# Delta-rule recurrence of an RWKV-7 layer: the doubling levels regrouped over the four quadrants of TensorE

## The reference

```python
def step(state, inp):
    r_t, w_t, k_t, v_t, kk_t, a_t = inp
    sa = jnp.einsum('bhvk,bhk->bhv', state, -kk_t)
    state = (state * w_t[:, :, None, :]
             + sa[..., None] * (kk_t * a_t)[:, :, None, :]
             + v_t[..., None] * k_t[:, :, None, :])
    y = jnp.einsum('bhvk,bhk->bhv', state, r_t)
    return state, y
...
_, y = lax.scan(step, state0, xs)
mu_y = jnp.mean(y, axis=-1, keepdims=True)
var_y = jnp.mean(jnp.square(y - mu_y), axis=-1, keepdims=True)
y = (y - mu_y) * lax.rsqrt(var_y + GN_EPS)
y = y * gn_g.reshape(H, N).astype(f32) + gn_b.reshape(H, N).astype(f32)
y = y + jnp.sum(rh * kh * r_k.astype(f32), axis=-1, keepdims=True) * vh
y = y.reshape(B, S, D).astype(h.dtype) * g
return y @ w_o
```

## Time and profile before

| what | value |
|---|---|
| median of 3 runs | 2886.83 us (2880.5 to 2887.5) |
| span of the profiled execution | 2890.0 us |
| level phases of the 8 pairs, first and last start of L3849 | 1697.1 and 2076.9 us |
| TensorE busy over the span | 2784.7 us (96%) |
| VectorE, GpSimd, ScalarE busy | 1962.0, 1435.9, 1370.0 us |

### The profile page before, as it was taken

The page is one execution under the profiler, slowest core; times in us unless marked ns, Lnnn a source line. Parts: engine busy times, 40 slices in busy tenths (PEclk is TensorE's granted clock), DMA queues, the critical chain, the costliest instruction groups (busy, mean ns, idle before and its releaser), DMA issues.

```text
span 2890.0 us, 63578 instructions
## 1 busy us (share of the span) xinstructions
PE 2784.7 (96%) x25936; PEld 2218.1 (77%) x25936; DVE 1962.0 (68%) x2814; ACT 1370.0 (47%) x2296; POOL 1435.9 (50%) x961
## 2 busy tenths in 40 slices
PE   8898899999999999998999999999999999999998
PEld 6544567887888888876678878988878788888887
DVE  6587888689777777788132347776647766656667
ACT  5476877235334433346433345666414443334445
POOL 0001000233777767774446636675552576677772
PEclk9899999999999999999999999999999999999999
DMA  8200000532332322331442411222312112111111
GB/s 300 77 1 16 1 2 2 212 106 62 88 102 73 93 81 83 93 113 32 160 146 88 161 60 55 76 85 64 112 36 59 44 48 69 44 44 58 57 45 73
DMA packets 194397, 225.29 MB, mean 78 GB/s; under 512 B 14862, under 2 KB 151649, under 8 KB 194209
## 3 DMA queue, kind: packets, MB, share of 16 engines
q1 hardware_dynamic: 182529, 180.66, 20.2%
q10 hardware_dynamic: 11680, 42.01, 4.0%
HBM read 185.15 MB, written 37.22 MB: 77 GB/s over the span
## 4 chain that ended last, share of the span: by engine, by line
PE 72%; DVE 9%; ACT 4%; issue 3%; POOL 2%; DMA 0%; ACTq 0%; DVEq 0%; SPq 0%; POOLq 0%
PE ps L148 18%; PE ps L149 18%; PE ps L150 18%; PE ps L3849 3%; DVE uc L1090 2%; PE ps L3858 2%; PE ps L2304 2%; PE ps L2293 1%; PE ps L2315 1%; PE ps L3778 1%; PE ps L3856 1%; ACT d_r L2446 1%; PE ps L3838 1%; DVE d_r L2706 1%; POOL w_lo L738 1%
## 5 line engine op out<-in xcount | busy, mean ns | idle before, releaser
L148 PE MATMUL ps<-x_hi,w_hi 128*128 128x512 f32 x1160 | 453.3, 391 | 2.9 <-POOL w_lo L738 2.8
L150 PE MATMUL ps<-x_hi,w_lo 128*128 128x512 f32 x1160 | 451.5, 389 | 0.0
L149 PE MATMUL ps<-x_lo,w_hi 128*128 128x512 f32 x1160 | 451.4, 389 | 0.0
L738 POOL TENSOR_TENSOR w_lo<-w_room,w_hi 128x512 fp32r<-128x512 f32 x188 | 287.7, 1543 | 232.4 <-ACT w_hi L1252 232.4
L738 POOL TENSOR_TENSOR w_lo<-sq_room,w_hi 128x512 fp32r<-128x512 f32 x182 | 285.8, 1581 | 218.9 <-ACT w_hi L1252 218.9
L1090 DVE SCALAR_TENSOR_TENSOR uc<-u,pc,uc 128x1024 f32<-128x1024 f32 x176 | 327.4, 1871 | 25.9 <-ACT uc L1266 15.6
L1078 DVE TENSOR_TENSOR u<-u,ps 128x512 f32<-128x512 f32 x228 | 151.1, 683 | 195.3 <-PE ps L150 170.9
L148 PEld LDWEIGHTS ps<-x_hi,w_hi 128*128 128x128 f32 x1160 | 217.7, 188 | 50.5 <-POOL w_lo L738 5.7
L148 PE MATMUL ps<-g_hi,w_hi 128*128 128x512 f32 x640 | 250.3, 391 | 6.5 <-DVE h L1156 6.2
L150 PEld LDWEIGHTS ps<-x_hi,w_lo 128*128 128x128 f32 x1160 | 217.7, 188 | 45.6
L149 PEld LDWEIGHTS ps<-x_lo,w_hi 128*128 128x128 f32 x1160 | 217.8, 188 | 44.8
(11 more groups left out here) (493 smaller groups left out, 6876.2 us busy)
## 6 DMA issues: line engine op xcount, KB each, us to landing
w_room<-in_f_w_up_dram SPq DMA_DIRECT2D x48, 512.0 KB, 5.0
rwkv_scratch<-rp_stage ACTq DMA_DIRECT2D x48, 512.0 KB, 3.5
sq_room<-in_f_w_up_dram SPq DMA_DIRECT2D x40, 512.0 KB, 4.6
ada_w<-in_ada_w_dram SPq DMA_DIRECT2D x80, 256.0 KB, 2.8
rc_raw<-rwkv_scratch SPq DMA_DIRECT2D x28, 512.0 KB, 3.9
d_ada_w<-in_ada_w_dram SPq DMA_DIRECT2D x24, 512.0 KB, 7.7
d_r<-in_ada_w_dram ACTq DMA_DIRECT2D x24, 512.0 KB, 6.4
sq_room<-in_f_w_down_dram SPq DMA_DIRECT2D x24, 512.0 KB, 4.4
```

The source lines that it names most:

```text
L148: pe.matmul(out, w_hi, x_hi, start=first, stop=False, skip_group_check=skip)
L149: pe.matmul(out, w_hi, x_lo, start=False, stop=False, skip_group_check=skip)
L150: return pe.matmul(out, w_lo, x_hi, start=False, stop=last, skip_group_check=skip)
L738: pool.tensor_tensor(slot_of(k.w_lo, s), src, slot_of(k.w_hi, s).bitcast(F32), ALU.subtract).then_inc(w_lo_done, 1)
```

## The change

It rearranges the levels. The second head's blocks 4 to 7 keep their l on the other partition half (`far`), so that the two halves of that head use different quadrants. A trip of TensorE's loop now has six groups of 16 matmuls, each over four quadrants: u and l of head 0 for blocks 0 to 3, the same for blocks 4 to 7, u of head 1, the next z of head 0 with l of head 1 for blocks 0 to 3, the same for blocks 4 to 7, and the next z of head 1. The loop is rotated: the first z stands ahead of it (`first_z`), the last u behind it (`last_u`), and it has four trips. ScalarE copies u and l of a whole head at a time, VectorE masks z of head 0 in two pieces and z of head 1 in one. Banks are dealt out anew, and so the sums of `kk*kk` go to halves of banks 2 and 3, and 5 and 6, and their reading (`max_dve`) stands ahead of the levels. On VectorE s1 moves behind level 1 and s2 behind level 4; on ScalarE `log_act` and `root_act` move from behind level 3 into level 5, between the copies of u of head 0 and head 1, and `turn_act` behind level 5. The diff, cut to its core:

```diff
     def max_dve(dve, q, i):
         dve.wait_ge(sem["sum"], 2 * q + i + 1)
-        dve.tensor_scalar(kk[:, halves(i)], bank(6 + i), 1e-24, None, ALU.max).then_inc(sem["max"], 1)
+        dve.tensor_scalar(kk[:, halves(i)].rearrange("p (b c) -> p b c", b=2), sums_of(q, i), 1e-24, None, ALU.max
+                          ).then_inc(sem["max"], 1)
...
         for i in range(2):
-            pe.matmul(bank(6 + i), same[:, :], kk[:, halves(i)], start=True, stop=True).then_inc(sem["sum"], 1)
+            if q >= 2 and i:
+                pe.wait_ge(sem["y_sb"], q - 1)
+            for n in range(2):
+                cols = slice((2 * i + n) * 2 * P, (2 * i + n + 1) * 2 * P)
+                last = pe.matmul(sums_of(q, i)[:, n, :], same[:, :], kk[:, cols], start=True, stop=True)
+            last.then_inc(sem["sum"], 1)
...
+    def far(h, x, c):
+        return c if h and x >= QUARTER else 1 - c
+
+    def z_of(pe, h, x, c):
+        i = x // QUARTER
+        out = bank(4 + i if h else 4 + 2 * i)[:, part(x, 1 - h if i == 0 else 0)]
+        return pe.matmul(out[hs(far(h, x, c)), :], tg[hs(c), x, h, G_M, :], ul[hs(c), 0, h, x, :],
+                         start=True, stop=True)
...
+    def first_z(pe, p):
+        for i in range(2):
+            if i and p + 1 < PAIRS:
+                pe.wait_ge(sem["max"], 2 * p + 4)
+            for x in quarter(i):
+                for c in range(2):
+                    a_last = z_of(pe, 0, x, 1 - c)
+                    if i:
+                        z_of(pe, 1, x, c)
+            a_last.then_inc(sem["z_ps"][0], 1)
+        pe.wait_ge(sem["z_sb"][0], 10 * p + 1)
+        for x in quarter(0):
             for c in range(2):
-                last = pe.matmul(bank(4 + h)[hs(1 - c), at(x)], tg[hs(c), x, h, G_M, :], ul[hs(c), 0, h, x, :],
-                                 start=True, stop=True)
-        last.then_inc(sem["z_ps"][h], 1)
+                last = z_of(pe, 1, x, c)
+        last.then_inc(sem["z_ps"][1], 1)
...
     def level_pe(pe, p, lv):
-        for h in range(2):
-            pe.wait_ge(sem["u_sb"][h], lv + 5 * p)
+        pe.wait_ge(sem["l_sb"][0], lv + 4 * p)
+        for i in range(2):
+            pe.wait_ge(sem["z_sb"][0], lv * 2 + (10 * p + i - 1))
+            pe.wait_ge(sem["l_sb"][1], lv * 2 + (8 * p + i - 1))
             begun(pe)
-            level_z(pe, h)
-        for h in range(2):
-            pe.wait_ge(sem["l_sb"][h], lv + 4 * p)
-            pe.wait_ge(sem["z_sb"][h], lv + 5 * p)
+            ul_a(pe, i)
+        pe.wait_ge(sem["z_sb"][1], lv + 5 * p)
+        begun(pe)
+        u_b(pe)
+        for i in range(2):
+            pe.wait_ge(sem["u_sb"][0], lv * 2 + (10 * p + i - 1))
             begun(pe)
-            level_ul(pe, h)
+            z_a_l_b(pe, i)
+        pe.wait_ge(sem["u_sb"][1], lv + 5 * p)
+        pe.wait_ge(sem["z_sb"][0], lv * 2 + (10 * p + 1))
+        begun(pe)
+        z_b(pe)
...
+            last_opened(pe, p)
             if p + 1 < PAIRS:
                 sums_pe(pe, p + 1)
...
             banks_opened(pe, p)
-            with pe.Fori(1, 6) as lv:
+            first_z(pe, p)
+            with pe.Fori(1, LV[-1]) as lv:
                 level_pe(pe, p, lv)
+            last_u(pe, p)
             if p + 1 < PAIRS:
                 bon_pe(pe, p + 1)
             tail_pe(pe, p)
...
             for lv in LV:
-                for s in range(2):
-                    levels_act(act, p, lv, s)
-                    if more and (lv, s) in ((1, 1), (2, 1)):
-                        ln_act(act, q, lv - 1)
-                    if p and (lv, s) == (3, 1):
-                        log_act(act, p - 1)
-                        root_act(act, p - 1)
-                    if more and (lv, s) in ((3, 1), (4, 1)):
-                        rs_act(act, q, lv - 3)
-                    if (lv, s) == (2, 1):
-                        turn_act(act, p, 0)
-                        turn_act(act, p, 1)
+                u_act(act, p, lv, 0)
+                if p and lv == LV[-1]:
+                    log_act(act, p - 1)
+                    root_act(act, p - 1)
+                u_act(act, p, lv, 1)
+                if lv < LV[-1]:
+                    la_act(act, p, lv)
+                    lb_act(act, p, lv)
+                if more and lv in (1, 2):
+                    ln_act(act, q, lv - 1)
+                if more and lv in (3, 4):
+                    rs_act(act, q, lv - 3)
+                if lv == LV[-1]:
+                    turn_act(act, p, 0)
+                    turn_act(act, p, 1)
             tail_act(act, p)
...
-            if p:
+            if more:
                 for i in range(2):
-                    s1_dve(dve, p - 1, i)
+                    max_dve(dve, q, i)
             for lv in LV:
-                for s in range(2):
-                    levels_dve(dve, p, lv, s)
-                    if more and (lv, s) == (1, 1):
-                        max_dve(dve, q, 0)
-                        max_dve(dve, q, 1)
-                    if p and (lv, s) == (3, 1):
-                        s2_dve(dve, p - 1, 0)
-                        s2_dve(dve, p - 1, 1)
-                    if p + 2 < PAIRS and (lv, s) == (2, 1):
-                        scan_dve(dve, p + 2, 0)
-                        scan_dve(dve, p + 2, 1)
+                for h in range(2):
+                    levels_dve(dve, p, lv, h)
+                if p and lv == 1:
+                    for i in range(2):
+                        s1_dve(dve, p - 1, i)
+                if p + 2 < PAIRS and lv in (2, 3):
+                    scan_dve(dve, p + 2, lv - 2)
+                if p and lv == 4:
+                    for i in range(2):
+                        s2_dve(dve, p - 1, i)
```

More of the change, by code:

```diff
@@ L101, in alloc @@
     k.nm_small = [k.sb(f"nm_small{i}", [P, 3, TT]) for i in range(3)]
-    k.ps = [stack.enter_context(nc.psum_tensor(f"ps{i}", [P, S], F32)) for i in range(4)]
+    k.ps_all = stack.enter_context(nc.psum_tensor("ps", [P, 4, S], F32))
+    k.ps = [k.ps_all[:, i, :] for i in range(4)]
     k.w_room = k.sb("w_room", [P, 2, S])
@@ L3800, in removed_pe @@
             for h in range(2):
[L3801 removed]
+                last = pe.matmul(g[hs(far(h, x, c)), h, 3 * C64:4 * C64], b_t[hs(h), toks(x, c)], ar[u][hs(h), x, 0, hs(c)],
                                  start=True, stop=True)
@@ new lines, in part, with u_of @@
+    def part(x, right=0):
+        return at(x % QUARTER + QUARTER * right)
+    def z_of(pe, h, x, c):
[3 more added lines that the diff above has]
+                         start=True, stop=True)
+    def u_of(pe, h, x, c):
+        side, i = hs(far(h, x, c)), x // QUARTER
+        out = bank(2 * h + i)[:, part(x)]
+        return pe.matmul(out[hs(c), :], ul[side, 1, h, x, :], z[side, h, x, :],
+                         start=False, stop=False, skip_group_check=True)
@@ new lines, in l_of, with quarter @@
+    def l_of(pe, h, x, c):
+        side = hs(far(h, x, c))
+        out = bank(x // QUARTER)[:, part(x, 1)] if h else bank(7)[:, at(x)]
+        return pe.matmul(out[side, :], z[side, h, x, :], ul[side, 1, h, x, :],
+                         start=False, stop=False, skip_group_check=True)
+    def quarter(i):
+        return range(QUARTER * i, QUARTER * (i + 1))
+    def first_z(pe, p):
[10 more added lines that the diff above has]
+        for x in quarter(0):
+            for c in range(2):
+                last = z_of(pe, 1, x, c)
+        last.then_inc(sem["z_ps"][1], 1)
@@ new lines, in ul_a, with u_b @@
+    def ul_a(pe, i, l_too=True):
+        for x in quarter(i):
+            for c in range(2):
+                u_last = u_of(pe, 0, x, c)
+                if l_too:
+                    l_last = l_of(pe, 0, x, 1 - c)
+        u_last.then_inc(sem["u_ps"][0], 1)
+        if l_too and i:
+            l_last.then_inc(sem["l_ps"][0], 1)
+    def u_b(pe):
+        for x in quarter(0):
+            for c in range(2):
+                u_of(pe, 1, x, c)
+                last = u_of(pe, 1, QUARTER + x, c)
+        last.then_inc(sem["u_ps"][1], 1)
@@ new lines, in z_a_l_b, with z_b, opened @@
+    def z_a_l_b(pe, i):
+        for x in quarter(i):
+            for c in range(2):
+                z_last = z_of(pe, 0, x, 1 - c)
+                l_last = l_of(pe, 1, x, c if i else 1 - c)
+        z_last.then_inc(sem["z_ps"][0], 1)
+        l_last.then_inc(sem["l_ps"][1], 1)
+    def z_b(pe):
+        for x in quarter(0):
+            for c in range(2):
+                z_of(pe, 1, x, 1 - c)
+                last = z_of(pe, 1, QUARTER + x, c)
+        last.then_inc(sem["z_ps"][1], 1)
+    def opened(pe, out, c, side_of):
+        pe.matmul(out[hs(c), at(0)], id64[hs(side_of), :], same[hs(side_of), hs(1 - side_of)],
+                  start=True, stop=False, skip_group_check=True)
@@ L3863, in banks_opened, with last_opened @@
+    def last_opened(pe, p):
+        pe.wait_ge(sem["g2_sb"], 2 * BLK * (p + 1))
+        if p:
+            pe.wait_ge(sem["s_sb"], UPD * p)
+        for c in range(2):
```

(25 more changed lines are left out.)

57 lines of the change are left out of this document (35 added, 22 removed).

## The result

The changed kernel takes 2947.79 us (median of four runs, 2941.41 to 2950.73), the kernel before on the same chip 2884.78: ratio 1.0211, 95% interval 1.0193 to 1.0229. It is 63 us slower, where 43 were forecast; it lies 3 us over the top of the range. The profiled execution has a span of 2944.2 us against 2890.0.

What follows compares the result with a forecast made beforehand. TensorE's issue was taken to bound the levels. First pair -1.2, six pairs +31.8, last +5.4, together +36, and clock +7 made +43 us: 2933 against 2890.0, or 2930 against the 2887 median; range 2905 to 2945.

Steps and rivals of the forecast that it cites:

- The root that comes later: Tail: late log and root delay TensorE's L3745 by 6.5 us in six pairs, 7.5 in the last (E: last u's end).
- The clock: Tails of seven pairs: TensorE's idle time lowers its clock, 1.0 us a pair, 7 in all, bounds 0 to 2.5.
- The levels: Level phases of each pair: regrouped matmuls take 20.7 us instead of 21.9, gaining 1.2 us, 2.1 in the last pair.
- The trip: One trip of TensorE's level loop: 3.95 us including waits for copies and the jump, where it was 4.20.
- The code: First trip of the loop: waiting for instructions left as before, 0.97 us a pair, with no term for added code.
- The other terms: Level phases, per pair: 2.0 us ahead of the loop, 1.4 behind it, 0.6 for delays by table loads.
- The signs: Expected in the trace: L3745 waits 4 us or more, two more loads a pair, trips 3.9 to 4.0, pairs 57 apart.
- Table sets: ScalarE: log and root each load a table, 3.04 us together, against the skill's rule of one load for both.
- the clock falls in the levels too: Rival, level phases: TensorE's waits in each trip lower the clock, 14 to 27 us more, 2944 to 2957; chance 0.12.
- The others: Rivals: fewer loads 2905 (0.10), copies covered 2909 (0.11), root off path 2876 (0.07), gain and loss cancel within 9 us (0.04).

## Why the prediction was right and wrong

**The root that comes later** was right, from ScalarE's copy to GpSimd's last operation: E + 10.4 was worked out and E + 10.2 measured, 6.5 us a pair and 6.45, 7.5 in the last pair and 7.5. Log and root took 3.03 us with both loads. u of head 1 and L4007 came at E + 3.9, as said.

**The clock** was named, with its place, and taken too small: 1.0 us a pair, 7 in all. From L3762 to the next pair it was 1.5 us more on average over six pairs (9.3 in all), and 4.3 behind the last pair's L3762; filling the idle time gave back 16 us in all, 2.3 a pair. It was within the bound of 2.5 that stood beside it. The reason for taking a low value, that part of what follows is VectorE's, does not hold: L4019 and the sums that wait for it stretch as well.

**The levels** are the step that failed. "The levels gain 1.2 us a pair", 10.5 us in all with the last pair; they gained nothing (175.0 against 174.2 us, where the terms give 164.3).
- *The trip* is the term that was mis-sized: 3.95 us in the sum, it was 4.24, over 32 trips 9 us. The mechanism was there (the next z waits for the copy of u, and z of head 1 for VectorE), and the run with u in halves shows it: without this wait it is 3.65. But in the third trip of the third pair the copy begins 1.26 us into the trip and not 1.2, the sixth group starts at 3.31 and not 3.15, and from there to the next trip there are 0.92 us, where 0.5 for the group and 0.3 for the jump were put.
- *The code*. "I leave this as it is", of the first trip: the fetching of instructions was taken as unchanged, although the rotated loop adds 64 matmuls of straight code to each pair. That this costs some 8 us is the estimate above. In the trace of after, the gaps without a releaser above 0.3 us sum to 10.7 us from the first block phase to L3762 of the last pair, against 7.7 in the kernel before (17.8 with the root put back), and the clock falls for 3.4 us right behind three of them (at 1721.4, 1748.7 and 2107.1 us). In the levels the allowance of 0.97 a pair covered most of it: the eight first trips together stand 8.4 us above 8 x 4.24, where 7.8 were allowed. The rest falls into the tails, a gap of 2.06 us ahead of L4041 in the first pair, of 1.61 in the last, for which the sum had no term. The row was there (5.17 against 4.20 us for the first trip), and I did not ask what more code would do to it.
- The other terms nearly cancel. The 24 later trips together stand 3.3 us above 24 x 4.24, with the table loads of ln and rs and two stretches of low clock in them, where 0.6 a pair was put for the loads. Ahead of the loop it is 1.8 us (put at 2.0), behind it 1.6 (put at 1.4).

**The 20 us between 43 and 63** can be added up from the two traces: 11.3 for the levels, 6.6 for the clock (9.3 and 4.3 against 7), 2.3 for the first pair's tail and 0.9 for the block phases, less 0.3 for the root. The 16 us that the filling gave back are near the 13.6 that the traces give for the clock.

**The signs.** Three came as said: the wait for L3748 in seven pairs, the loads at log and rs, and the clock below 1.00 in the tails. Three did not: the longest of these waits is 3.0 us and not 4 or more, since L4007 filled part of the time at the low clock; the trips are 4.24 us apart and not 3.9 to 4.0; and the pairs are 59.6 us apart, where 57 were forecast and 51.5 are the kernel before's.

**Table sets.** In the trace of after each logarithm that follows an exponential loads, and each exponential that follows a logarithm: log loads all eight times (L3722), six of them behind rs and two behind the root of the pair before. The Trainium skill (ScalarE: Activation LUTs, Table sets: the hidden batching unit) has one set with exp and ln both, so that ln and then exp need one load; the trace decides against it here. The Trainium skill (ScalarE: Activation LUTs, What ACT_TABLE_LOAD costs) gives about 1283 ns for the load itself; the trace has 1.28 us, and of the drain that it adds, nothing: the next operation starts 0.01 to 0.02 us behind.

Of the **rivals**, the one that the clock falls in the levels too came true in part: a stretch of 3.4 us at 1.2 GHz lies in the levels of the second pair and one in those of the last. The others did not: log and root load each time, the trip is 4.24 us and not 3.3, and L3762 stands at E + 10.2.

## What to carry to other kernels

When an instruction moves later in one engine's list, follow its consumer through every engine to the place where the bound engine waits, and compare with the slack there; here 2.1 us of slack met 8.7 us of delay, and two operations of 0.2 us cost 48 us. Shortening a loop takes the cover from everything that ran beside it (copies, table loads), so a copy should be as fine as the group that waits for it. And straight code is not free where instructions are short: price the added instructions by the packets in which they arrive, about 250 instructions each, at 1.0 us a packet (12 packets) to 1.6 (37 packets) here.

## What was not expected

- Code as a bound: writing out three trips a pair more cost 59 us (2887 to 2947), and 384 instructions a pair cost 12 us.
- The clock: 26 matmuls a pair whose results nobody reads made the kernel 16 us faster, since TensorE stayed at 2.4 GHz, though its transposes came no earlier.
- In these traces VectorE and GpSimd slow each other on float32 tensors in SBUF: with rs behind the root, L3606 takes 2.37 us a piece beside `gain`, where it takes 0.74 in the changed kernel, and GpSimd's operations 2.68 in place of 2.35 us. The kernel before had this too (L3594 with a mean of 1.67 us), hidden.

What stays open: how much of the first trip's gap is the packet and how much the clock behind it, and whether the six groups without extra code (the loop not rotated) would beat the kernel before; that was not tried, since the grouping of z with l of head 1 needs the rotation.
